# Both heads' value products in one, a seven-product down projection, and a join step cut in two

## The reference

```
for each layer:
    p_l, p_c = modulate(rms_norm(x or xc)) @ w_in
    oa = grouped-query attention;  ob = attention over low-rank keys and values
    oc = recurrent mixer (two directions);  od = neighbourhood attention with a bias
    x = x + gate1 * (sum_i sigmoid(g_i) * (o_i @ w_branch_i)) @ w_out
    x = x + gate2 * (square(relu(h @ w1)) @ w2)        # w1: 1024 x 4096, w2: 4096 x 1024
    the same for xc, except in the last layer
return rms_norm(x, g_final)
```

## Time and profile before

| | |
|---|---|
| median of 3 runs | 2406.4 us (2401.82 to 2408.03) |
| the profiled execution | 2408.26 us, of it a span of 2406.5 us |
| PE busy | 2362.7 us, 98% |
| DVE, ACT, POOL busy | 1075.4, 602.9, 348.2 us |
| mean granted clock of PE | 0.994 of full |

### The profile page before, as it was taken

How to read it: one execution, slowest core, us unless ns; L and a number is a source line. 1 busy time by engine, 2 the same in 40 slices (tenths; PEclk the granted TensorE clock), 3 DMA queues, 4 the chain that set the end, 5 groups by cost and what they waited for, 6 DMA issues and landing times.

```text
span 2406.5 us, 48804 instructions
## 1 busy us (share of the span) xinstructions
PE 2362.7 (98%) x21774; PEld 1617.1 (67%) x21774; DVE 1075.4 (45%) x1988; ACT 602.9 (25%) x1248; POOL 348.2 (14%) x249
## 2 busy tenths in 40 slices
PE   8999999999999999999999999999999999999998
PEld 5554564455556554458888887566577767788887
DVE  3452334243555542137876875431546566421101
ACT  3353323132232321011000002441333334211100
POOL 0000000000101100026666671010000011000000
PEclk9999999999999999999999999999999999999999
DMA  8101111213231113232224565112121212245443
GB/s 307 53 18 70 45 61 44 96 63 110 95 107 39 45 46 115 78 123 97 88 88 149 189 243 194 53 71 89 53 89 64 64 61 66 81 149 175 155 152 105
DMA packets 64543, 239.99 MB, mean 100 GB/s; under 512 B 7024, under 2 KB 8064, under 8 KB 63440
## 3 DMA queue, kind: packets, MB, share of 16 engines
q1 hardware_dynamic: 61824, 220.23, 26.6%
q0 software_dynamic: 2512, 16.66, 1.9%
HBM read 235.81 MB, written 1.05 MB: 98 GB/s over the span
## 4 chain that ended last, share of the span: by engine, by line
PE 89%; DVE 5%; DMA 2%; issue 1%; ACT 1%; SPq 0%; DVEq 0%; ACTq 0%
PE psum L430 87%; PE psum L769 2%; DMA normed<-panels 1%; DVE normed L2348 1%; DVE normed L2345 1%; DMA arena<-panels 1%; DVE arena L2329 0%; SPq L2712 0%; ACT arena L811 0%; DVE arena L1492 0%; ACT normed L719 0%; ACT arena L821 0%; DVE arena L1509 0%; DVE arena L1507 0%; DVE arena L1235 0%
## 5 line engine op out<-in xcount | busy, mean ns | idle before, releaser
L430 PE MATMUL psum<-normed,panel_ring 128*128 128x256 f32 (+1 forms) x2880 | 973.5, 484 | 3.0 <-DVE arena L1235 1.1
L430 PEld LDWEIGHTS psum<-normed,panel_ring 128*128 128x128 f32 x2880 | 530.2, 190 | 318.9 <-issue 265.8
L430 PE MATMUL psum<-arena 64*64 64x64 f32 (+6 forms) x14040 | 608.2, 251 | 20.1 <-issue 9.0
L430 PEld LDWEIGHTS psum<-arena 64*64 64x64 f32 (+3 forms) x14040 | 431.6, 139 | 251.6 <-issue 180.9
L430 PE MATMUL psum<-arena,panel_ring 128*128 128x256 f32 (+1 forms) x2048 | 550.4, 422 | 0.0
L430 PEld LDWEIGHTS psum<-arena,panel_ring 128*128 128x128 f32 x2048 | 384.3, 190 | 125.2 <-issue 81.4
L786 DVE TENSOR_REDUCE softmax_stats<-psum 128x1 f32<-128x512 f32 (+1 forms) x144 | 83.7, 599 | 171.6 <-PE psum L430 170.3
L811 ACT ACTIVATE arena<-psum,softmax_stats 128x512 f32<-128x512 f32 (+1 forms) x144 | 87.6, 612 | 211.8 <-PE psum L769 102.5
L1235 DVE SCALAR_TENSOR_TENSOR arena<-arena,psum 128x512 f32<-128x512 f32 (+1 forms) x64 | 35.3, 553 | 152.8 <-PE psum L430 145.3
L1220 ACT ACTIVATE arena<-psum 128x512 f32<-128x512 f32 (+1 forms) x64 | 31.4, 490 | 216.1 <-PE psum L430 216.0
L1728 POOL COPY arena<-arena 128x512 f32<-128x512 f32 x16 | 21.3, 1356 | 440.8 <-PE psum L430 431.1
(11 more groups left out here) (215 smaller groups left out, 1872.5 us busy)
## 6 DMA issues: line engine op xcount, KB each, us to landing
panel_ring<-panels SPq DMA_DIRECT2D x350, 512.0 KB, 3.5
normed<-panels SPq DMA_DIRECT2D x40, 512.0 KB, 3.7
arena<-panels SPq DMA_DIRECT2D x24, 512.0 KB, 12.0
arena<-small_b POOLq DMA_DIRECT2D x2, 2176.0 KB, 8.9
arena<-bias_d POOLq DMA_DIRECT2D x2, 2048.0 KB, 8.9
arena<-x_t SPq DMA_DIRECT2D x2, 1024.0 KB, 7.1
arena<-x_t POOLq DMA_DIRECT2D x1, 2048.0 KB, 10.6
arena<-const_r POOLq DMA_DIRECT2D x2, 800.0 KB, 6.3
```

The costliest lines, as they stand in the source:

```text
L430: return nc.tensor.matmul(out, lhsT, rhs, start=start, stop=stop, skip_group_check=check)
```

## The change

Three edits. In the attentions the two value products of a key tile become one call: stationary 128 keys x 128 value columns (both heads), moving 512 columns (both heads' probabilities). Half of each result is of use, the diagonal blocks; DVE copies these out in two instructions of 64 partitions. In layer 1, `stage_mlp` is replaced by `stage_mlp_down7`: the up panels stay as they are, and the down projection is done in 16 units of two panels; each unit is seven products of four calls with 128 columns. POOL makes three of the weight sums of a unit and DVE two, and DVE forms the sums of the hidden tiles; four times, after every fourth unit, ACT and DVE join the seven sums into four quarter tiles (`join`). In the mixer the join's last step becomes two: first `kt` and `vt`, then `bt` and `pu`, `h_full`, and behind it the products for `yb`; JOIN is 4, so the same other work is spread over 25 instead of 24 steps, and half of a tick's share of it comes ahead of the close and prep steps.

```diff
--- before.py
+++ after.py
-PREP, RAW, LEVEL_STEPS, JOIN, SCAN, CLOSE = 17, 4, 2 * (LEVELS - 1), 3, NCH - 1, 8
+PREP, RAW, LEVEL_STEPS, JOIN, SCAN, CLOSE = 17, 4, 2 * (LEVELS - 1), 4, NCH - 1, 8
 CORE_FILL = [2] * (RAW + LEVEL_STEPS + JOIN + SCAN)
...
                     for kt in range(nk // P):
-                        for i in range(2):
-                            p = mm(psum[heads[i], 4 + g % 2, :CTX], v_of(t, i, kt), probT[:, g % 2, i, kt, :], kt == 0, kt == nk // P - 1)
+                        p = mm(psum[:, 4 + g % 2, :], v_of(t, kt), probT[:, g % 2, :, kt, :], kt == 0, kt == nk // P - 1)
                     p.then_inc(pv_done.h, 1)
...
-                    nc.vector.tensor_copy(out[:, t, half * CTX - col0:(half + 1) * CTX - col0], psum[:, 4 + g % 2, :CTX]).then_inc(out_free.h, 1)
+                    for i in range(2):
+                        p = nc.vector.tensor_copy(out[heads[i], t, half * CTX - col0:(half + 1) * CTX - col0],
+                                                  psum[heads[i], 4 + g % 2, i * CTX:(i + 1) * CTX])
+                    p.then_inc(out_free.h, 1)
                 yield
...
-            e.wait_ge(gq_ready.h, gq_ready.at(1))
-            for c in y_chunks:
-                for d, hd in units:
-                    t = tside(d, hd)
-                    mm(yb[d][half[hd], token(c)], pu[t, d, c, 1, :], m4[t, d, c, :], False, False, check=True)
             for n, (src, right) in enumerate(((kt, vt), (bt, pu[:, :, :, 1, :]))):
+                if n == 0:
+                    e.wait_ge(gq_ready.h, gq_ready.at(1))
                 for c in range(NCH):
                     for d, hd in units:
                         t = tside(d, hd)
                         if c != order[d][-1]:
                             p = mm(psum[half[hd], d, token(c)], src[t, d, c, :], right[t, d, c, :], n == 0 and c == 0, n == 1, check=True)
-            p.then_inc(h_full.h, 1)
-            yield
+                if n == 1:
+                    p.then_inc(h_full.h, 1)
+                    for c in y_chunks:
+                        for d, hd in units:
+                            t = tside(d, hd)
+                            mm(yb[d][half[hd], token(c)], pu[t, d, c, 1, :], m4[t, d, c, :], False, False, check=True)
+                yield
...
                 p.then_inc(gq_ready.h, 1)
             yield
+            yield
             e.wait_ge(h_full.h, h_full.at(1))
...
-    def stage_mlp(l, tok, hid, relu, ready, acc):
+    def stage_mlp_down7(l, tok, at, ready):
...
+        half = n // 2
+        left, right = slice(tok.start, tok.start + half), slice(tok.start + half, tok.stop)
...
+        opens = lambda u: u % 4 == 0
+        closes = lambda u: u % 4 == 3
...
-            for m in range(KT):
-                ps = outs.take(e)
-                for q in range(4):
-                    w, slot_in, n_in = stream.take(l, P_DOWN + 4 * m + q)
-                    e.wait_ge(slot_in.h, n_in)
-                    for k in range(KT):
-                        if m == 0:
-                            e.wait_ge(hid_ready.h, hid_ready.at(8 * q + k + 1))
-                        p = mm(ps[:, :n], w[:, k, :], hid[:, 8 * q + k, :n], q == 0 and k == 0, q == 3 and k == 7)
-                        if k == 0:
-                            p.then_inc(panels_begun.h, 1)
-                p.then_inc(outs.full.h, 1)
-                yield
...
+            def product(u, out, lhs, part, opening, begins=False):
+                for k in range(4):
+                    p = mm(out, lhs[:, k, :], hid[:, 4 * (u % 4) + k, part, :], opening and k == 0, closes(u) and k == 3, check=True)
+                    if begins and k == 0:
+                        p.then_inc(panels_begun.h, 1)
+                return p
+
+            for u in range(NU):
+                at_first = P_DOWN + 8 * (u // 4) + u % 4
+                loaded[u] = stream.take(l, at_first), stream.take(l, at_first + 4)
+            for u in range(NU):
+                v, x2, x5, x1 = u // 4, wx[:, u % 2, 1], wx[:, u % 2, 2], wx[:, u % 2, 0]
+                (w1, _, _), (w2, _, _) = loaded[u]
+                if v == 0:
+                    e.wait_ge(hid_ready.h, hid_ready.at(summed_at(4 * u + 3)))
+                if opens(u) and v >= 2:
+                    e.wait_ge(emptied.h, emptied.at(v - 1))
+                e.wait_ge(weights.h, weights.at(3 * u + 1))
+                product(u, bank(v, 0)[:, 1, :], x2, 0, opens(u))
+                e.wait_ge(shared.h, shared.at(2 * u + 1))
+                product(u, bank(v, 1)[:, 0, :], x5, 3, opens(u))
+                p = product(u, bank(v, 0)[:, 0, :], w1[:, 0:4, :], 1, False, begins=True)
+                if closes(u):
+                    p.then_inc(m3_full.h, 1)
+                e.wait_ge(shared.h, shared.at(2 * u + 2))
+                product(u, bank(v, 2)[:, 0, :], w1[:, 4:8, :], 6, opens(u))
+                e.wait_ge(weights.h, weights.at(3 * u + 3))
+                p = product(u, bank(v, 1)[:, 1, :], w2[:, 4:8, :], 2, False, begins=True)
+                if closes(u):
+                    p.then_inc(m4_full.h, 1)
+                p = product(u, bank(v, 2)[:, 1, :], w2[:, 0:4, :], 5, False)
+                if closes(u):
+                    p.then_inc(m67_full.h, 1)
+                product(u, m1_bank(v), x1, 4, opens(u)).then_inc(m1_done.h, 1)
+                yield
+            e.wait_ge(added.h, added.at(KT - 3))
+            token_sums(6, h[:, 0, tok], n, True)
+            e.wait_ge(squared.h, squared.at(KT - 1))
+            token_sums(6, h[:, KT - 2, tok], n, False)
+            e.wait_ge(squared.h, squared.at(KT))
+            token_sums(6, h[:, KT - 1, tok], n, False).then_inc(sums_full.h, 1)
+            yield
+
+        def arrived(e, u):
+            for _, slot_in, n_in in loaded[u]:
+                e.wait_ge(slot_in.h, n_in)
+            if u >= 2:
+                e.wait_ge(m1_done.h, m1_done.at(u - 1))
+
+        def pool(e):
+            yield from idle(8 * N_UP)
+            for u in range(NU):
+                (w1, _, _), (w2, _, _) = loaded[u]
+                arrived(e, u)
+                nc.gpsimd.tensor_tensor(wx[:, u % 2, 1], w2[:, 0:4, :], w2[:, 4:8, :], ALU.add).then_inc(weights.h, 1)
+                nc.gpsimd.tensor_tensor(w2[:, 0:4, :], w2[:, 0:4, :], w1[:, 0:4, :], ALU.subtract).then_inc(weights.h, 1)
+                nc.gpsimd.tensor_tensor(wx[:, u % 2, 0], w1[:, 0:4, :], w2[:, 4:8, :], ALU.add).then_inc(weights.h, 1)
+                yield
             yield
...
+                if closes(u):
+                    c, spare = cx[:, v % 2, 0:4, :], cx[:, v % 2, 4:6, :]
+                    e.wait_ge(m3_full.h, m3_full.at(v + 1))
+                    nc.scalar.activation(spare, bank(v, 0), ACT.Copy).then_inc(m3_copied.h, 1)
+                    e.wait_ge(m67_full.h, m67_full.at(v + 1))
+                    nc.scalar.activation(c[:, ::3, :], bank(v, 2), ACT.Copy).then_inc(m67_copied.h, 1)
+                    e.wait_ge(residual_done.h, residual_done.at(2 * v + 1))
+                    nc.scalar.activation(h[:, 2 * v, right], x[:, 2 * v, right], ACT.Square)
+                    nc.scalar.activation(h[:, 2 * v + 1, left], x[:, 2 * v + 1, left], ACT.Square)
+                    e.wait_ge(residual_done.h, residual_done.at(2 * v + 2))
+                    nc.scalar.activation(h[:, 2 * v, left], x[:, 2 * v, left], ACT.Square).then_inc(squared.h, 1)
+                    e.wait_ge(emptied.h, emptied.at(v + 1))
+                    nc.scalar.activation(h[:, 2 * v + 1, right], x[:, 2 * v + 1, right], ACT.Square).then_inc(squared.h, 1)
...
+            def weight_sums(u):
+                (w1, _, _), (w2, _, _) = loaded[u]
+                arrived(e, u)
+                nc.vector.tensor_tensor(wx[:, u % 2, 2], w1[:, 0:4, :], w1[:, 4:8, :], ALU.add).then_inc(shared.h, 1)
+                e.wait_ge(shared.h, shared.at(2 * u + 1))
+                nc.vector.tensor_tensor(w1[:, 4:8, :], w1[:, 4:8, :], w2[:, 4:8, :], ALU.subtract).then_inc(shared.h, 1)
...
+                if second:
+                    e.wait_ge(hid_ready.h, hid_ready.at(squared_at(j)))
+                    two = s[:, 0:4, :].rearrange("p (a b) t -> p a b t", a=2)
+                    nc.vector.tensor_tensor(s[:, 5:7, :], two[:, :, 0, :], two[:, :, 1, :], ALU.add)
+                    link(e, nc.vector.tensor_tensor(s[:, 4, :], s[:, 0, :], s[:, 3, :], ALU.add))
+                    nc.vector.tensor_tensor(s[:, 1:3, :], s[:, 1:3, :], s[:, 3::-3, :], ALU.subtract).then_inc(hid_ready.h, 1)
+                if j in (29, 31):
...
+            def join(v):
+                c, spare, m1_part = cx[:, v % 2, 0:4, :], cx[:, v % 2, 4:6, :], m1_bank(v)
+                e.wait_ge(m3_copied.h, m3_copied.at(v + 1))
+                e.wait_ge(m4_full.h, m4_full.at(v + 1))
+                link(e, nc.vector.tensor_tensor(c[:, 1:3, :], spare, bank(v, 1), ALU.add))
+                residual_of(2 * v, 1, c[:, 1, :])
```

(79 more changed lines are left out.)

17 lines of the change are left out of this document (7 added, 10 removed).

## The result

The changed kernel takes 2448.53 us (median of 4, 2446.85 to 2450.41) against 2407.22 of the kernel before: ratio 1.0177, 95% interval 1.0159 to 1.0194, 41 us slower. The forecast was 2441, 35 us slower, with a range of 2430 to 2452.

The account below looks back on a forecast made before the run. PE was taken to bound the kernel, busy 2362.7 of 2406.5 us. Terms +46.0 - 9.2 - 2.0 = +34.8 on the profiled 2408.26 us gave 2443.1, as a median 2441; range 2430 to 2452.

Parts of the forecast that it names:

- The bound: Whole kernel: PE has no slack, so every us of matmul stream added or removed moves the end.
- Part 1: Attentions' value products: 480 records of 256 columns become 240 of 512 at 0.43 us; net +46.0 us, at most +50.6.
- Rival C: Attentions' 36 groups of value products: the merged call is not dearer than the pair; kernel at 2390, at break-even 2395; chance 0.05.
- The 0.14 us on top of a group: Attentions' old value products: each group costs 0.14 us beyond its records, already counted in the 57.2 us removed.
- Part 2: Layer 1's down projection: products take 100.4 us instead of 110.5, the tail grows; together -9.2 us.
- the tail: End of layer 1's down projection: more work between the last product and the last sums, +0.9 us (0.5 to 1.8).
- A: Layer 1's down projection: weight sums come late and PE follows POOL; 8 us more, 2449; chance 0.09.
- D: Layer 1's down projection: 128-column products stall on the waits between them, the whole saving is lost; 2451; chance 0.06.
- Part 3: Mixers: the split join step and moved fill steps can win PE's waits; -2 us, from +3 to -10.
- Rival B: Mixers: the regrouped steps remove the stall and low-clock stretch and more like it; -10 instead of -2, 2433; chance 0.08.

Follow-up runs that it names:

- pv_same_half: The kernel before with both heads' value products in the same half of the array, same order, DVE copying out in two instructions: 2456.7 us, ratio 1.0213.
- down7_only: The kernel before with layer 1's seven-product down projection alone: 2395.5 us against 2403.5, ratio 0.9967.
- pv_only: The kernel before with the merged value products alone, DVE copying out in two instructions: 2454.5 us against 2403.5, ratio 1.0204.
- down7_sums_on_pool: The kernel before with the seven-product down projection and all five weight sums of a unit on POOL: 2393.2 us against 2403.5, ratio 0.9955.

## Why the prediction was right, and where it was off

**The bound.** Right: no slack on PE. The added stream of the attentions came through whole, in the change and by itself (+45.9 by the marks).

**Part 1.** 0.43 us per merged record (eight in 3.43), 1.55 and 0.71 us more per group: 24 x 1.55 + 12 x 0.71 = 45.7 against 46.0. The reason given, two half-width products side by side, is shown by `pv_same_half`: take only the second half away, and the old records cost as much as the merged ones (3.59 and 3.43 us per group). Rival C had its price from equal useful work; the array's time goes by columns that stream, whether half the result is of use or not. The 0.14 us on top of a group are real and small: they stand in the half-width groups also when one half is used alone (1.88 less 8 x 0.216), and the merged groups lack them (3.43 against 8 x 0.43). That they are the change of the array's mode was not tested apart.

**Part 2.** Products 100.05 us against 100.4 forecast; the tail +1.28 us (1.84 to 3.12 us from the last product to L668) against +0.9; together -9.2 against -9.2. The agreement to a tenth is luck in that the two errors, 0.35 and 0.4 us, cancel. Rivals A and D are out: a unit lasts 6.26 us, and even five sums on POOL do not hold it up. The tail's row shows what was left out of the term: DVE still has the second of the two sums for M6 and M7 before it when M1 is done, and the pair of residuals that needs M1 starts 1.3 us after it. Two slips of the text changed nothing: seven products for eight are an eighth less arithmetic, and 0.112 less 0.108 is 4 ns per record, not 5.

```profile
2438.23 0.42 DVE L2115 TENSOR_TENSOR arena<-arena,psum 128x256 f32<-128x256 f32 x1
...
2439.33 0.61 DVE L2096 SCALAR_TENSOR_TENSOR arena<-psum,modulation,arena 128x128 f32<-128x128 f32 x2
```

**Part 3.** This is the step that failed, in sign: -2 forecast, +5.8 measured (3.4 to 8.2), outside the term's own bounds of -10 to +3. The prediction asked which wait a step ahead of prep would lift, and that wait did shrink: at the same place it is 1.8 us instead of 2.7, and in total those for L1235 fall from 3.8 to 1.8. (Directly ahead of that L1235 DVE does prep's L1507 and L1509, 1.22 us each; the earlier trace rows do not show them.) That waits may turn up elsewhere stands in the prediction as a bound and has no place in the sum: PE waits more for the scan's DVE (3.2 to 6.5) and newly for prep's tanh on ACT (1.7), and a wait of 1.3 us for L1770 is gone. These waits net make only 1.7 us. The rest of the 5.8 lies in PE's "issue" waits and its busy time, and its cause is open. In size the term explains the miss: 2441 + 7.8 = 2449. Rival B, which had the same edit at -10, is out by the same runs.

The parts measured alone add to 49 - 8 + 6 = 47 us, the change to 43 (38 to 47) by its ratio; the intervals of the parts are wide enough for that.

**The range.** The prediction says that it goes from B to D with part 1's own bounds. That would be 2433 - 1 = 2432 to 2451 + 4.6 = 2456, and not 2430 to 2452. The result lies in both, though part 3 came out beyond its own bounds: the room that A and D were given took it in.

**A caution on single profiles.** Kernels with the same code up to layer 1's MLP differ by 5 us in layer 0's mixer. Two rows of the same stretch, PE busy and granted clock, first of the kernel before, then of `down7_only`:

```profile
584.00:628.00 44.00, 39.99 (x615) 0.88 0.32 121
```
```profile
584.00:628.00 44.00, 39.86 (x719) 0.96 0.37 133
```

PE stops there for 4 us in both, with the same wait of 2.7 us for L1235, but the clock is 0.88 in the first and 0.96 in the second. So the low clock of the earlier trace rows comes with that wait in one execution more than in another, and its 2 us were no firm part of what lifting the wait could win. The trace of before is the odd one: from the mixer's first mark to its last it takes 509.4 us, five of the six other traces with this mixer unchanged take 503.7 to 504.4 (`pv_only` 510.7), and the changed kernel takes 507.6. The -1.7 us of layer 0's mixer in the comparison of traces is therefore no gain of the change; only the timed runs decided part 3. Likewise one wait for DVE's residual in layer 0's MLP, code that no edit touches, is 5.0 and 4.1 us in the traces of `down7_only` and `down7_sums_on_pool`, 0.7 in that of the whole change and at most 1.3 in the others; its cause is open.

## What to carry to other kernels

Count PE's work by streamed columns per half of the array: here two products of 64 stationary columns in different halves took one product's time, so merging them into one of 128 columns with a moving side of twice the length doubled it. Splitting a large product into seven smaller ones still paid at 128 moving columns (9.5% of the stream, not 12.5), with the sums made a unit ahead. When filler work is moved to lift one wait, list the waits of the steps around it as well, give what may take its place a term of the sum, and decide by timed runs of that edit alone.

## What the runs showed of the hardware

Half-width products need not alternate strictly: four records of one half in a row cost 0.02 to 0.05 us per group, eight cost 0.9 us per group of 16.

DVE and POOL hold each other up when both add two SBUF tiles. In the changed kernel's timeline at the start of the down projection, DVE's additions of 128x256 and 128x128, 0.42 and 0.28 us in all fourteen cases each without POOL beside them, last as long as the POOL sum beside them. POOL's first sum of a unit goes from 1.27 us to as much as 1.79. That one engine waits for the other's whole instruction would fit these lengths; it is not shown apart.

```profile
2328.47 1.33 POOL L2039 TENSOR_TENSOR arena<-panel_ring 128x512 f32<-128x512 f32 x1 [233.55 <-DMA panel_ring<-panels]
2328.71 1.37 DVE L2087 TENSOR_TENSOR arena<-arena 128x256 f32<-128x256 f32 x1
2329.77 1.45 POOL L2040 TENSOR_TENSOR panel_ring<-panel_ring 128x512 f32<-128x512 f32 x1
2330.01 1.35 DVE L2088 TENSOR_TENSOR arena<-arena 128x128 f32<-128x128 f32 x1
```

A product of 128x128 by 128 columns with fresh weights each time spaces at 0.112 us, 4 ns above half of a 256-column one, also when PE waits for POOL's and DVE's sums between every few of them (56 in 6.26 us).
